# Layer norm of the convolution module in four pairs, attention's next maximum ahead of recurrence operations, and another order in the recurrence's tail

## The reference

```python
uf = u.astype(jnp.float32)
mu = jnp.mean(uf, axis=-1, keepdims=True)
var = jnp.mean(jnp.square(uf - mu), axis=-1, keepdims=True)
u = ((uf - mu) * lax.rsqrt(var + EPS) * ln_g + ln_b).astype(h.dtype)
return jax.nn.silu(u) @ w_pw2 + b_pw2
```

```python
s = jnp.einsum('bqhd,bkhd->bhqk', qi, k).astype(jnp.float32) * scale
pr = jax.nn.softmax(s, axis=-1).astype(v.dtype)
o_attn = jnp.einsum('bhqk,bkhd->bqhd', pr, v)

# recurrence, per chunk and direction
scores = jnp.einsum('bthk,btshk,bshk->bhts', qc, decay, kc)
o = jnp.einsum('bhts,bshv->bthv', scores, vc) + jnp.einsum(
    'bthk,bhkv->bthv', qc * jnp.exp(bcum), state)
# readout: norm of o, times the gain, times silu(gate)
y = jnp.concatenate([attn, hg, fn], axis=-1) @ w_out[l]
```

## Time and profile before

| | us |
|---|---|
| median of 3 runs (1112.51, 1113.61, 1115.98) | 1113.61 |
| the profiled execution | 1115.49 |
| its span in the trace | 1113.7 |
| PE busy | 1051.3 (94%) |
| DVE busy | 644.4 (58%) |
| ACT busy | 506.8 (46%) |
| POOL busy | 68.5 (6%) |
| granted PE clock, mean share of full speed | 0.974 |

### The profile page before, as it was taken

One profiled execution on the slowest core, in us unless ns is written; L12 is line 12 of the kernel. 1 busy time (PEld: TensorE's weight loads), 2 busy tenths in 40 slices (PEclk: granted clock), 3 DMA queues, 4 the chain that ended last, 5 costly groups with the idle time before them and its releaser, 6 DMA issues.

```text
span 1113.7 us, 16603 instructions
## 1 busy us (share of the span) xinstructions
PE 1051.3 (94%) x7158; PEld 909.9 (82%) x7158; DVE 644.4 (58%) x709; ACT 506.8 (46%) x575; POOL 68.5 (6%) x84
## 2 busy tenths in 40 slices
PE   7998999999999997999999998999898879999997
PEld 6996888888888784988888887898557768888886
DVE  5656548666676552657776554353558654444544
ACT  6467454444445233644444443454456444444332
POOL 0001200000000000000010000000226000000000
PEclk9999999999999998899999999999989889999999
DMA  6541447666762774347788554222000335555451
GB/s 259 194 172 51 179 159 251 230 239 226 245 213 84 238 230 142 121 181 269 265 298 288 182 180 179 109 93 97 1 1 2 115 116 187 189 188 176 170 183 39
DMA packets 34046, 187.69 MB, mean 169 GB/s; under 512 B 3776, under 2 KB 8128, under 8 KB 15296
## 3 DMA queue, kind: packets, MB, share of 16 engines
q1 hardware_dynamic: 25920, 155.66, 39.5%
q0 software_dynamic: 7200, 27.27, 7.2%
q10 hardware_dynamic: 864, 3.88, 0.9%
HBM read 181.09 MB, written 1.05 MB: 164 GB/s over the span
## 4 chain that ended last, share of the span: by engine, by line
PE 86%; DVE 5%; ACT 4%; DMA 2%; issue 1%; SPq 1%; POOL 0%; DVEq 0%; ACTq 0%
PE PS L269 12%; PE PS L271 12%; PE PS L270 12%; PE PS L534 11%; PE PS L535 11%; PE PS L536 11%; PE PS L997 2%; DMA raw<-wstream 1%; PE PS L434 1%; PE PS L547 1%; PE PS L298 1%; PE PS L299 1%; PE PS L300 1%; DMA U<-CU 1%; ACT w_hi L252 1%
## 5 line engine op out<-in xcount | busy, mean ns | idle before, releaser
L256 DVE TENSOR_TENSOR w_lo<-raw,w_hi 128x2048 fp32r<-128x2048 f32 x140 | 320.6, 2292 | 223.3 <-ACT w_hi L252 223.3
L252 ACT ACTIVATE w_hi<-raw 128x2048 fp32r<-128x2048 f32 x141 | 269.1, 1911 | 209.4 <-PE PS L271 103.2
L534 PE MATMUL PS<-w_hi,a_hi 128*128 128x512 f32 x528 | 211.7, 401 | 4.4 <-DVE a_lo L460 4.2
L535 PE MATMUL PS<-w_lo,a_hi 128*128 128x512 f32 x528 | 208.2, 394 | 0.0
L536 PE MATMUL PS<-w_hi,a_lo 128*128 128x512 f32 x528 | 208.2, 394 | 0.0
L269 PE MATMUL PS<-a_hi,w_hi 128*128 128x256 f32 (+1 forms) x608 | 187.5, 308 | 15.5 <-DVE a_lo L1897 5.0
L271 PE MATMUL PS<-a_hi,w_lo 128*128 128x256 f32 (+1 forms) x608 | 182.9, 301 | 0.0
L270 PE MATMUL PS<-a_lo,w_hi 128*128 128x256 f32 (+1 forms) x608 | 182.8, 301 | 0.0
L269 PE MATMUL PS<-h_hi,w_hi 128*128 128x256 f32 x528 | 149.9, 284 | 0.4 <-DVE h_lo L699 0.4
L271 PE MATMUL PS<-h_hi,w_lo 128*128 128x256 f32 x528 | 149.4, 283 | 0.0
L270 PE MATMUL PS<-h_lo,w_hi 128*128 128x256 f32 x528 | 149.4, 283 | 0.0
(11 more groups left out here) (304 smaller groups left out, 1085.9 us busy)
## 6 DMA issues: line engine op xcount, KB each, us to landing
raw<-wstream SPq DMA_DIRECT2D x142, 1024.0 KB, 4.9
modraw<-wmod POOLq DMA_DIRECT2D x48, 512.0 KB, 5.0
U<-CU SPq DMA_DIRECT2D x32, 142.0 KB, 4.5
cst<-cst ACTq DMA_DIRECT2D x1, 1632.0 KB, 9.9
mlw<-mlw ACTq DMA_DIRECT2D x1, 1280.0 KB, 5.8
X<-xT SPq DMA_DIRECT2D x2, 512.0 KB, 5.3
CROW<-crow POOLq DMA_DIRECT2D x1, 1024.0 KB, 5.2
CTX<-ctxT POOLq DMA_DIRECT2D x1, 1024.0 KB, 8.5
```

Source lines behind the costliest of these rows:

```text
L252: nc.scalar.activation(w_hi[:, slot, :], raw[:, rslot, :], ACT.Copy).then_inc(S("hi_done"), 1)
L256: dve.tensor_tensor(w_lo[:, slot, :], raw[:, rslot, :], w_hi[:, slot, :].bitcast(F32), ALU.subtract).then_inc(S("lo_done"), 1)
L534: nc.tensor.matmul(out, a_hi[:, k, src, ts], wh, start=k == 0, stop=False, skip_group_check=True)
L535: nc.tensor.matmul(out, a_hi[:, k, src, ts], wl, start=False, stop=False, skip_group_check=True)
```

## The change

1. Convolution norm: DVE subtracts in four operations of two tiles, ACT squares in four of two tiles, PE waits for each pair. ACT's `ctx_factor` comes after the squares instead of before them.
2. DVE, attention loop: `ml_max(0)` stands before the loop, and `ml_max(i + 1)` right after the scaling of pass i, ahead of that pass's recurrence operations.
3. DVE: the two multiplications of the gate by its gain (`hgg`, L2125) move from the tail to before the loop.
4. DVE, tail: `hg_gated_queries(1)` moves from after `hg_states(1)` to after `hg_states(0)`; `lo(U_OUT2)` moves behind the last `pair_copy`.
5. PE, tail: level 4 of direction 1 moves from before the clearing and the state products to after them.

No instruction is added or taken out but for the two subtractions and two squares that come from cutting.

```diff
--- before.py
+++ after.py
@@ -1019,7 +1019,7 @@
                 i = nc.tensor.matmul(PS[:, 6, 0:T], ones, HN[:, k, :], start=k == 0, stop=k == KT - 1)
             i.then_inc(S("ln_sum"), 1)
             for k in range(KT):
-                pe.wait_ge(S("ln_sq"), k // 4 + 1)
+                pe.wait_ge(S("ln_sq"), k // 2 + 1)
                 i = nc.tensor.matmul(PS[:, 6, T:2 * T], ones, SQ[:, k, :], start=k == 0, stop=k == KT - 1)
             i.then_inc(S("ln_ss"), 1)
             out_units_pe(pe, U_PW2, "cv", 2, 1)
@@ -1236,8 +1236,8 @@
             hg_level(1, 0)
             hg_level(1, 1)
             hg_update(1)
-            for l in range(2, 5):
-                hg_level(1, l)
+            hg_level(1, 2)
+            hg_level(1, 3)
 
             def hg_out(n, h):
                 return PS[half(h % 2), 2 + n % 2, (h // 2) * T + n * 64:(h // 2) * T + n * 64 + 64]
@@ -1253,6 +1253,7 @@
                             nc.tensor.matmul(hg_out(n, h), SX[:, d, n, h * 64:h * 64 + 64],
                                              QF[:, d, h * T + n * 64:h * T + n * 64 + 64],
                                              start=False, stop=False, skip_group_check=True)
+            hg_level(1, 4)
             hg_level(1, 5)
             pe.wait_ge(S("hg_copied"), 13)
             for a in range(2):
@@ -1440,11 +1441,11 @@
             table(LN_EXP)
             act.wait_ge(S("ln_sum"), 1)
             nc.scalar.activation(MU, PS[:, 6, 0:T], ACT.Copy, scale=1.0 / D).then_inc(S("ln_a"), 1)
+            for j in range(4):
+                act.wait_ge(S("ln_d"), j + 1)
+                nc.scalar.activation(SQ[:, 2 * j:2 * j + 2, :], HN[:, 2 * j:2 * j + 2, :], ACT.Square)\
+                    .then_inc(S("ln_sq"), 1)
             ctx_factor(act)
-            for j in range(2):
-                act.wait_ge(S("ln_d"), j + 1)
-                nc.scalar.activation(SQ[:, 4 * j:4 * j + 4, :], HN[:, 4 * j:4 * j + 4, :], ACT.Square)\
-                    .then_inc(S("ln_sq"), 1)
             act.wait_ge(S("ln_ss"), 1)
             nc.scalar.activation(RS, PS[:, 6, T:2 * T], ACT.Ln, scale=1.0 / D, bias=prm_eps).then_inc(S("ln_a"), 1)
             act.wait_ge(S("ln_a"), 2)
@@ -1883,9 +1884,9 @@
 
             dve.wait_ge(S("cv_read"), KT)
             dve.wait_ge(S("ln_a"), 1)
-            for j in range(2):
-                ks = slice(4 * j, 4 * j + 4)
-                dve.tensor_tensor(HN[:, ks, :], HN[:, ks, :], MU.unsqueeze(1).to_broadcast([P, 4, T]), ALU.subtract)\
+            for j in range(4):
+                ks = slice(2 * j, 2 * j + 2)
+                dve.tensor_tensor(HN[:, ks, :], HN[:, ks, :], MU.unsqueeze(1).to_broadcast([P, 2, T]), ALU.subtract)\
                     .then_inc(S("ln_d"), 1)
             dve.wait_ge(S("ln_a"), 3)
             for k in range(KT):
@@ -2034,6 +2035,10 @@
             dve.tensor_tensor(KPE[:, 0:T], KPE[:, 0:T], KPE[:, T:2 * T], ALU.add).then_inc(S("rope"), 1)
             dve.wait_ge(S("rope"), 5)
             dve.tensor_copy(KPE[:, T:2 * T], CKV[:, 1, T:2 * T]).then_inc(S("rope_done"), 1)
+            dve.wait_ge(S("hg_z"), 1)
+            for a in range(2):
+                i = dve.tensor_scalar(XO[:, 6 + a, :], XO[:, 6 + a, :], prm("hgg", a), None, ALU.mult)
+            i.then_inc(S("hg_g"), 1)
 
             def ml_max(i):
                 dve.wait_ge(S("ml_s"), i + 1)
@@ -2062,13 +2067,15 @@
                                     PS[:, 6 + g % 2, :].rearrange("p (m t) -> p m t", m=8))\
                     .then_inc(S("hg_copied"), 1)
 
+            ml_max(0)
             for i in range(8):
-                ml_max(i)
                 dve.wait_ge(S("ml_exp"), i + 1)
                 dve.reciprocal(MXS[:, 16 + i:17 + i], MXS[:, 8 + i:9 + i]).then_inc(S("ml_rc"), 1)
                 dve.wait_ge(S("ml_rc"), i + 1)
                 dve.tensor_scalar(PR[:, i % 2, :], PR[:, i % 2, :], MXS[:, 16 + i:17 + i], None, ALU.mult)\
                     .then_inc(S("ml_p"), 1)
+                if i < 7:
+                    ml_max(i + 1)
 
                 if i == 0:
                     hg_exclusive()
@@ -2109,23 +2116,19 @@
             pair_copy(0, 6)
             pair_queries(1, 1)
             hg_states(0)
+            hg_gated_queries(1)
             pair_copy(1, 0)
             pair_queries(1, 2)
             pair_copy(1, 1)
             pair_queries(1, 3)
             hg_states(1)
-            hg_gated_queries(1)
             pair_copy(1, 2)
             pair_queries(1, 4)
             pair_copy(1, 3)
             pair_queries(1, 5)
-            lo(dve, U_OUT2)
-            dve.wait_ge(S("hg_z"), 1)
-            for a in range(2):
-                i = dve.tensor_scalar(XO[:, 6 + a, :], XO[:, 6 + a, :], prm("hgg", a), None, ALU.mult)
-            i.then_inc(S("hg_g"), 1)
             pair_copy(1, 4)
             pair_copy(1, 5)
+            lo(dve, U_OUT2)
             mix_split_lo(dve, 1, (0, 1))
 
             dve.wait_ge(S("hg_r"), 1)
```

## The result

| | before | changed |
|---|---|---|
| median, us (7 runs each) | 1113.61 (1109.75 to 1115.98) | 1105.17 (1101.98 to 1110.6) |
| profiled execution, us | 1115.49 | 1105.17 |
| its span | 1113.7 | 1103.4 |
| mean granted PE clock in it | 0.974 | 0.98 |

The ratio is 0.9914, with a 95% interval of 0.9891 to 0.9937: 9.6 us less (7.0 to 12.1). The medians of the table are 8.4 us apart and the means 7.6, both inside that interval. The forecast was 9.4 less, 1105.0. The total was met, but not by its terms: in the profiles the loop gave less than forecast, norm and tail more.

What follows compares the result with a forecast made beforehand. PE, 86% of the chain, was taken as the bound, losing time only in pauses or at low clock. Norm 1.0, loop 7.0 and tail 1.4 summed to 9.4 us, forecast 1105.0, range 1100.5 to 1110.0.

Steps and rivals of the forecast that it cites:

- Norm, pause 1.0: Convolution norm: with half-size first subtraction and square, PE starts the sums of squares 1.0 us sooner; bounds 0.6 to 1.1.
- Maximum ahead, pause 3.1: Attention loop: the second maximum no longer waits behind `hg_exclusive`, so PE's key transpose starts 3.1 us earlier.
- if the clock stays up: Attention loop: PE at full clock reaches pass 2's transpose 6.3 us earlier, 3.1 from the pause and 3.2 from the clock.
- rival A: Attention loop: the clock falls all the same, loop gains 2.8 us, total 5.2, time 1109.2; chance 0.26.
- the main case: Whole kernel: norm 1.0, attention loop 7.0 with the clock up, tail 1.4, sum 9.4 us; chance 0.45.
- Later pauses: Attention passes 6 and 7: PE's pauses of about 0.3 and 0.23 us for the maximum vanish, 0.6 us more.
- No wait of over 0.5 us for scores from pass 3 on: Attention loop: DVE waits over 0.5 us for scores from pass 3 on would show the sum wrong.
- Tail, order 1.4: Tail: state products ahead of level 4 let PE end at 868.75 instead of 870.14, 1.4 us; bounds -0.5 to 2.2.
- The upper bound of 2.2: Tail: gain of up to 2.2 us if the state products run at 2.4 GHz.
- rival C: Norm: clock doesn't fall, 3.2 us more, 12.6 in all, 1101.8; similar if the tail's low stretch goes; chance 0.15.
- B: After the loop: its gain is not passed on, only 2.7 us remain, time 1111.7; chance 0.10.
- D: Attention loop: clock falls and stays low until the loop's end, 30 us, time 1120.0; chance 0.04.

Runs made afterwards that it cites:

- the cut alone: Norm's subtractions, squares and waits cut into four, context factor left ahead of the squares, against the kernel before: 1109.53 us, one time only.
- tail alone: Tail's reordering with gated queries, output-unit conversion and gate moved, against the kernel before: ratio 0.9985 (0.9966 to 1.0003), 1.7 us less.
- this part alone: Only the convolution norm's four pairs and context factor behind the squares, against the kernel before: ratio 0.9999 (0.9984 to 1.0014).
- the maximum alone: Only attention's maximum moved one pass ahead on VectorE, against the kernel before: ratio 0.9961 (0.9941 to 0.9981), 4.3 us less.
- the gate late: Changed kernel with zero matmuls in six TensorE pauses and the gate moved ahead of the third maximum: ratio 0.9876 against the kernel before, median 1101.42 us.
- the second profile: The changed kernel run once more, unedited, against the kernel before: ratio 0.9917 (0.9894 to 0.994), 9.3 us less.

## Why the prediction was right, and where it was not

- **Norm, pause 1.0: right**, 0.96 or 0.97 in every profile of the new order, and the cut alone, in its one execution, gave all of it. At full clock the segment is 11.94 us in the old order (tail alone) and 10.98 in the new. The rest of the 2.04 us in the two profiles is clock. That no gain in time could be measured for this part alone keeps it to the profile. Full clock in the sums was put at 3.2 us; it is worth 6.49 - 3.72 = 2.8.
- **Maximum ahead, pause 3.1: right.** 3.12 with the maximum alone, 2.81 in the changed kernel. The missing 0.31 is the gate's move, which I costed at nothing because VectorE had 2.27 us to spare. VectorE had; GpSimd had not. The two gate operations took 1.38 us instead of 0.61 and made GpSimd's clearings longer, its exponents came that much later, and the first scaling ended later with them. The scaling starts 4.58 us after the first scores in both kernels. It ends 0.28 us after GpSimd's operation in both (803.30 and 803.02, 800.79 and 800.51), and 0.29 after it with the gate late (804.12 and 803.83), so it waits for the rest of that operation. The gate's second operation likewise ends 0.14 us after the first clearing does (796.01 and 795.87). `hg_exclusive` ends 2.15 us after GpSimd's fourth exponent operation in both kernels and shrank from 3.19 to 2.59 us, while an operation of the same size clear of GpSimd took 2.28; so some of the 3.1 us that I read as VectorE's work was this wait. The Trainium skill (SBUF — State Buffer, "Who interferes with whom") says that such an operation with a scalar can hold the port that GpSimd uses and block it fully. The trace agrees: the waiting operation is held until its neighbour's end, and it lost tenths only where the neighbour was nearly through.
- **Loop, "if the clock stays up": this step failed.** It put 3.2 us on the vanished low stretch. The clock fell all the same, 9.1 us after the first scores (before 9.2), and for 6.8 us instead of 10.2. In these two profiles that saved next to nothing: at full clock the old order reaches the end of the first states in 53.58 us (3.4 less than measured), the new one in 49.33 (3.3 less). The old stretch began in the pause, where no work suffered; the new one is all work. Its length is not the same in each execution: 6.8 us in three of the four profiles with the new order and no zeros, 3.4 in the one with the maximum alone; 10.2 in five of six with the old order, 6.8 in the one of the tail alone. So rival A was nearer in mechanism. It gave 2.8 for the loop, the main case 7.0, measured 4.37.
- **Later pauses: sized too small.** From the transpose of pass 2 to the last values it was 23.33 us, now 22.07: 1.26, not 0.6 (at full clock in both orders 23.99 and 22.07). After it 0.5 is lost again, 12.26 to 12.74 us from the last values to the end of the first states, where exponents, ScalarE and VectorE take turns. Without the low clock order and pause come to 53.58 - 49.33 = 4.25 us.
- **No wait of over 0.5 us for scores from pass 3 on: wrong as a test.** VectorE waits 0.9 to 1.8 us there in three of four passes, with cover to spare; TensorE has no pauses. The cover of three microseconds held.
- **Tail, order 1.4: right in size** (1.43 at equal clock), wrong in its account. "It gives the tail nothing by itself" and "no cost" for the conversion hid that these two together had to leave for the copies to come sooner. The upper bound of 2.2, for products at 2.4 GHz, was too low: the clock gave 1.5 more, 2.93 in all. That 1.5 is no luck: the state products were at full clock in every profile of the new order and in none of the old one without zeros. The forecast had it only as an upper bound and as a case of rival C. The fear that gated queries under GpSimd would cost up to 1.48 did not come true on TensorE's path: they took 1.61 us against 1.22, GpSimd's operation beside them took 2.50 us where its like took 1.51, and neither VectorE nor level 2 waited for it.
- **Rivals.** B (not passed on) fell with the maximum alone. C's mechanism, full clock in the norm's sums, occurred in the second profile. D did not occur: the loop's low stretches were 3.4 to 6.8 us in the new order. The total was right because the loop's missing 2.6 us were made up by 1.0 in the norm and 1.5 in the tail, both clock (that in the norm by chance of the execution as far as is known, that in the tail with the order), and another 1.0 in the segments that no edit touches. That the total fits this closely is partly luck: the loop's error was covered by terms that the main case did not count.

## What to carry to other kernels

When a pause of TensorE is shortened, count the clock by the work that will stand in its low stretch, not by the length of the stretch: a pause that shrinks but still lets the clock fall may give back little more than the pause. Compare segments at equal clock before crediting an order with a gain, and fill a pause with matmuls of zeros to separate the two. An operation that is moved into an engine's idle time can still cost the neighbour that runs beside it, and an operation left in the way can cancel a better order elsewhere.

## What the runs showed of the hardware

Matmuls of zeros in bf16 held TensorE's clock up: with them there was no low stretch in the loop (three kernels of the new order and one of the old), in the state products of the tail (two of the new and one of the old), or in the norm (two). Six of them, 1.3 us, were worth 3 us. Identical instructions ran largely at 1.2 GHz in one profiled execution and at 2.4 in the next (the norm's sums of squares, 5.41 and 3.72 us), and the fastest and the slowest of the changed kernel's first seven runs, 8.6 us apart, had mean granted clocks of 0.983 and 0.977, which is 6.6 us of it.
